# The last down projection of a two-model transformer kernel as seven block products in two passes, with the block sums on GpSimd

## What is computed

```
h2 = _rmsnorm(x, g_ffn[l])
z = _dwconv(h2 @ w_up[l], w_dw_ffn[l], b_dw_ffn[l])      # 2 * 2816 channels, taps -1, 0, +1 over tokens
zg, zv = jnp.split(z, 2, axis=-1)
x = x + (jax.nn.silu(zg) * zv) @ w_down[l]               # (512 x 2816) by (2816 x 1024)
...
return _rmsnorm(x, g_final)
```

## Time and profile before

| | |
|---|---|
| median of 3 runs | 1885.44 us (1885.15 to 1885.94) |
| span of the profiled execution (first to last instruction) | 1883.8 us; its own time outside the span is not given, the median of the runs lies 1.6 us above the span |
| busy: PE, DVE, ACT, POOL | 99%, 62%, 49%, 4% |
| last down projection on PE | 1754.2 to 1877.4 us, 123.2 us |
| last matmul started to end of span | 1877.2 to 1883.8 us |

### The profile page before, as it was taken

How to read it: one execution, slowest core, us unless ns; L and a number is a source line. 1 busy time by engine, 2 the same in 40 slices (tenths; PEclk the granted TensorE clock), 3 DMA queues, 4 the chain that set the end, 5 groups by cost and what they waited for, 6 DMA issues and landing times.

```text
span 1883.8 us, 27086 instructions
## 1 busy us (share of the span) xinstructions
PE 1861.2 (99%) x8985; PEld 1504.1 (80%) x8985; DVE 1165.4 (62%) x2030; ACT 917.1 (49%) x1685; POOL 75.4 (4%) x110
## 2 busy tenths in 40 slices
PE   8999999999999999999999999999999999999998
PEld 7888888888888877677888888888757878888887
DVE  6877765733333377776566666336777576666534
ACT  6777654543433353666544434334456553444433
POOL 1111000000000000100200000000010020000000
PEclk9999999999999999999999999999999999999999
DMA  5222232333333324521333333333441223333333
GB/s 153 69 79 79 76 104 79 101 95 100 95 98 97 95 73 102 108 53 35 101 95 95 95 95 105 96 95 88 118 83 43 68 81 109 95 95 95 96 95 106
DMA packets 169241, 171.33 MB, mean 91 GB/s; under 512 B 48563, under 2 KB 123329, under 8 KB 169153
## 3 DMA queue, kind: packets, MB, share of 16 engines
q1 hardware_dynamic: 169048, 170.16, 31.5%
q10 hardware_dynamic: 104, 0.03, 0.0%
HBM read 159.25 MB, written 2.10 MB: 86 GB/s over the span
## 4 chain that ended last, share of the span: by engine, by line
PE 91%; DVE 5%; ACT 2%; issue 1%; DMA 0%; SPq 0%; DVEq 0%; ACTq 0%
PE bank_b L2457 16%; PE bank_b L2458 16%; PE bank_b L2459 16%; PE bank_a L2457 11%; PE bank_a L2458 11%; PE bank_a L2459 11%; PE bank_b L2959 2%; PE bank_b L3063 2%; PE bank_a L3044 1%; DVE w_lo L1535 1%; DVE arena L1538 1%; DVE arena L1535 1%; PE bank_a L2482 1%; PE bank_a L2485 1%; PE bank_a L2488 1%
## 5 line engine op out<-in xcount | busy, mean ns | idle before, releaser
L1535 DVE TENSOR_TENSOR w_lo<-w_raw,w_hi 128x512 fp32r<-128x512 f32 (+2 forms) x621 | 412.3, 675 | 535.3 <-ACT w_hi L1264 327.4
L1264 ACT ACTIVATE w_hi<-w_raw 128x512 fp32r<-128x512 f32 (+3 forms) x396 | 232.9, 599 | 435.6 <-PE bank_b L2459 222.2
L2457 PE MATMUL bank_b<-h_hi,w_hi 128*128 128x512 f32 (+1 forms) x952 | 372.7, 391 | 1.9 <-DVE h_lo L1538 0.8
L2459 PE MATMUL bank_b<-h_hi,w_lo 128*128 128x512 f32 (+1 forms) x952 | 369.0, 388 | 0.0
L2458 PE MATMUL bank_b<-h_lo,w_hi 128*128 128x512 f32 (+1 forms) x952 | 369.0, 388 | 0.0
L901 ACT ACTIVATE w_hi<-w_raw 128x512 fp32r<-128x512 f32 x225 | 137.7, 627 | 227.6 <-PE bank_b L2459 116.9
L2457 PEld LDWEIGHTS bank_b<-h_hi,w_hi 128*128 128x128 f32 x952 | 178.8, 188 | 41.2 <-issue 3.1
L2458 PEld LDWEIGHTS bank_b<-h_lo,w_hi 128*128 128x128 f32 x952 | 178.8, 188 | 37.0 <-issue 1.4
L2459 PEld LDWEIGHTS bank_b<-h_hi,w_lo 128*128 128x128 f32 x952 | 178.7, 188 | 36.6
L2457 PE MATMUL bank_a<-h_hi,w_hi 128*128 128x512 f32 x513 | 200.6, 391 | 0.3
L2458 PE MATMUL bank_a<-h_lo,w_hi 128*128 128x512 f32 x513 | 199.5, 389 | 0.0
(11 more groups left out here) (314 smaller groups left out, 2665.3 us busy)
## 6 DMA issues: line engine op xcount, KB each, us to landing
w_raw<-in_w_up_dram SPq DMA_DIRECT2D x240, 256.0 KB, 3.1
w_raw<-in_w_down_dram SPq DMA_DIRECT2D x152, 256.0 KB, 2.6
arena<-arena SPq DMA_DIRECT2D x32, 268.0 KB, 4.2
w_raw<-in_w_in_dram SPq DMA_DIRECT2D x64, 128.0 KB, 2.3
w_raw<-in_w_gate_dram SPq DMA_DIRECT2D x32, 256.0 KB, 2.8
w_raw<-in_w_in_dram SPq DMA_DIRECT2D x32, 256.0 KB, 2.6
w_raw<-in_w_o_dram SPq DMA_DIRECT2D x32, 256.0 KB, 2.6
w_raw<-in_w_out_dram SPq DMA_DIRECT2D x16, 256.0 KB, 2.7
```

The lines of the kernel that those rows point to most:

```text
L1264: nc.scalar.activation(w_hi[:, s, 0:c], w_raw[:, s, 0:c], ACT.Copy).then_inc(w_round, 1)
L1535: return nc.vector.tensor_tensor(out_, a, b, op)
L2457: nc.tensor.matmul(out_, a_hi, b_hi, start=start, stop=False, skip_group_check=loose)
L2459: return nc.tensor.matmul(out_, a_lo, b_hi, start=False, stop=stop, skip_group_check=loose)
```

## The change

The down projection is written as a product of 2x2 blocks. Rows: tokens 0 to 255 and 256 to 511. Columns: the two halves of 512. The contraction is taken in 11 pairs q of chunks (2q, 2q+1). With x11, x21 the two token halves of `act2` tile 2q, x12, x22 those of tile 2q+1, and w11, w12, w21, w22 the four weight chunks of the pair, seven products of sums take the place of eight products of blocks. Each product is a chunk by two token tiles, so 6 matmuls; before, each of the eight blocks of a pair was that too.

- **Two passes.** PSUM holds only four accumulators of two banks (`acc_x`, `acc_v`, `acc_z`, `acc_y`). Pass 1 runs the products w11, t3, t2, t1 of all q, pass 2 w21, t4, w22. The order of all 77 products is `DOWN_ORDER`. Between the passes and within the second the accumulators are copied or added into SBUF (`copy_bank` on ACT, `tensor_copy` and `tt` on DVE, four adds on GpSimd). The residual is no longer put in first: four visits of eight transposes use `acc_y` in pass 2 and DVE adds them.
- **Sums on GpSimd.** `act_sums` makes three sums of 128x256 for each pair q out of `act2` (the ones of q = 0 to 8 during the up projection), `weight_sums` three of 128x512 for each q (t3 and t1 in place in the raw buffers, t2 into freed tiles), `second_sums` one of 128x256 and one of 128x512 for each q in pass 2.
- **Factors.** A factor is rounded by ACT (`round_factor`) and its rest made by DVE (`rest_factor`) into a ring of 8 slots instead of 4; an activation operand likewise (`round_unit`, `rest_unit`), still four slots. In pass 1 the units are two of 128x512 for each q, in pass 2 one of 128x512 and one of 128x256.
- **Loads.** 55 loads of 256 KB in place of 44 (w22 is loaded in both passes), into two raw buffers for each of w11, w12 and w22. A raw buffer is loaded again when the factor in it is split and t2 of that q is made (`pass1_freed`).
- **The last group's** FFN tiles are made between factors, its outer taps at q = 2 to 5 and its product at q = 6.
- **The end.** Token tiles 2 and 3 are finished first, then 0 and 1. Each output tile is a DVE add of PSUM and SBUF (`end_sum`) ahead of the squares, which now read SBUF.
- Semaphores are merged (`act_made`, `dve_set`, `raw_land`) with the same order of work.

```diff
+DP = F2T // 2
+HS = S // 2
+RING = 8
+PASS1, PASS2 = ("w11", "t3", "t2", "t1"), ("w21", "t4", "w22")
+DOWN_ORDER = ([(kind, q) for kinds in (PASS1[:2], PASS1[2:]) for q in range(2) for kind in kinds]
+              + [(kind, q) for q in range(2, DP) for kind in PASS1]
+              + [(kind, q) for kind in PASS2 for q in range(2)]
+              + [(kind, q) for q in range(2, DP - 2) for kind in PASS2]
+              + [("t4", DP - 2), ("t4", DP - 1)] + [(kind, q) for q in range(DP - 2, DP) for kind in ("w21", "w22")])
...
@@ sync
+            def pass1_freed(kind, q):
+
+                sp_.wait_ge(w_split, d0 + DOWN_AT[(kind, q)] + 1)
+                sp_.wait_ge(t_made, 3 * q + 3)
...
+            for q in range(DP):
+                for src, dst, slot, kind in ((last_down[:, 2 * q, 0, :], raw11, q % 2, "w11"),
+                                             (last_down[:, 2 * q, 1, :], raw12, q % 2, "t1"),
+                                             (last_down[:, 2 * q + 1, 1, :], raw22, 2 + q % 2, "t3")):
+                    if q >= 2:
+                        pass1_freed(kind, q - 2)
...
+                    sp_.dma_start(dst[q % 2], src).then_inc(raw_land[slot], 16)
@@ gpsimd
+            def act_sums(q):
+
+                x11, x21, x22 = act2[:, 2 * q, 0:HS], act2[:, 2 * q, HS:S], act2[:, 2 * q + 1, HS:S]
+                pool.wait_ge(a_ready, was[a_ready.name] + 2 * q + 2)
...
+                nc.gpsimd.tensor_tensor(s13_of[q][:, 0:HS], x21, x22, ALU.add).then_inc(s_made, 1)
+                nc.gpsimd.tensor_tensor(s13_of[q][:, HS:S], x11, x21, ALU.subtract).then_inc(s_made, 1)
+                pool.wait_ge(s_made, 3 * q + 2)
+                nc.gpsimd.tensor_tensor(x21, s13_of[q][:, 0:HS], x11, ALU.subtract).then_inc(s_made, 1)
+
+            def weight_sums(q):
...
+                nc.gpsimd.tensor_tensor(raw22[b], raw22[b], raw12[b], ALU.subtract).then_inc(t_made, 1)
+                pool.wait_ge(t_made, 3 * q + 1)
+                nc.gpsimd.tensor_tensor(raw12[b], raw12[b], raw11[b], ALU.subtract).then_inc(t_made, 1)
+                if q < 2:
+                    pool.wait_ge(w_split, d0)
+                else:
+                    pool.wait_ge(w_used, d0)
+                nc.gpsimd.tensor_tensor(t2_of[q], raw22[b], raw11[b], ALU.add).then_inc(t_made, 1)
+
+            def second_sums(q):
...
+                nc.gpsimd.tensor_tensor(act2[:, 2 * q, 0:HS], act2[:, 2 * q + 1, 0:HS], act2[:, 2 * q, HS:S],
+                                        ALU.subtract).then_inc(s_made, 1)
...
+                nc.gpsimd.tensor_tensor(raw12[r % 2], raw11[r % 2], t2_of[q], ALU.subtract).then_inc(t_made, 1)
...
+            for q in range(DP - 2):
+                act_sums(q)
+            weight_sums(0)
+            act_sums(DP - 2)
+            for q in range(1, DP):
+                weight_sums(q)
+                if q == DP - 3:
+                    act_sums(DP - 1)
@@ vector
+            for u in range(4):
+                rest_unit(u)
+            for kind, q in DOWN_ORDER[0:6]:
+                rest_factor(kind, q)
+            dve.wait_ge(w_used, d0)
+            for j in range(4):
+                tt(zp[:, j, 1:1 + S], bank_b[:, j, :], rstd[:, 1, :], ALU.mult).then_inc(z_out, 1)
+            for kind, q in DOWN_ORDER[6:8]:
+                rest_factor(kind, q)
+            for q in range(2, DP):
+                for kind in PASS1:
+                    rest_factor(kind, q)
+                for b in range(2):
+                    rest_unit(2 * q + b)
+                if 2 <= q < 6:
+                    for j in range(2):
+                        last_tap_of(2 * (q % 2) + j, 2 * (q // 4))
...
@@ tensor
+            def product(kind, q, acc, tiles, start, stop):
...
+                pe.wait_ge(w_split, d0 + n + 1)
+                pe.wait_ge(as_ready, before(DEPTH2 - 1)[as_ready.name] + u + 1)
+                for t in tiles:
+                    c = slice(first + t * P, first + t * P + P)
+                    last = mm3(acc[:, t, :], as_hi[:, u % 4, c], as_lo[:, u % 4, c], ring_hi(n), ring_lo(n), start, stop, True)
+                return last
...
+            def down_tokens(emptied):
...
+                for n, (kind, q) in enumerate(DOWN_ORDER[0:4 * DP]):
+                    if n == 4:
+                        pe.wait_ge(z_out, emptied + 4)
+                    product(kind, q, accs[kind], range(2), q == 0, q == DP - 1).then_inc(w_used, 1)
```

More of the change, by code:

```diff
@@ L1524, in _ @@
-            for t in range(TT):
-                for half in range(2):
-                    act.wait_ge(yt_made, 2 * t + half + 1)
-                    nc.scalar.activation(y_sq[:, 2 * t + half, :], y_bank(t, half), ACT.Square,
-                                         accum_out=tok[:, half, t:t + 1]).then_inc(tok_sq, 1)
-                tokens_guess(t, slice(t, t + 1))
+                act_pair(split2, act2, M_END - 4, F2T - 2, was["a_ready"])
+                for n in range(2):
+                    split_layer(l + 1, n)
@@ new lines, in _ @@
+            round_factor("w22", 1)
+            copy_bank(sum_p7, acc_v, ("t3", DP - 1))
+            for b in range(2):
+                round_unit(2 * DP + 2 + b)
+            for q in range(2, DP - 2):
+                for kind in PASS2:
+                    round_factor(kind, q)
+                for b in range(2):
+                    round_unit(2 * (DP + q) + b)
+                if q == 4:
+                    for t in range(2):
+                        act.wait_ge(yt_made, t + 1)
+                        nc.scalar.activation(sum_r[:, t, :], acc_y[:, t, :], ACT.Copy).then_inc(bank_copied, 1)
@@ new lines, in _, with token_square @@
+            for kind, q in (("t4", DP - 2), ("t4", DP - 1), ("w21", DP - 2), ("w22", DP - 2)):
+                round_factor(kind, q)
+            for q in range(DP - 2, DP):
+                for b in range(2):
+                    round_unit(2 * (DP + q) + b)
+            for kind in ("w21", "w22"):
+                round_factor(kind, DP - 1)
+            def token_square(src, half, t):
+                nc.scalar.activation(y_sq[:, 2 * t + half, :], src, ACT.Square,
+                                     accum_out=tok[:, half, t:t + 1]).then_inc(tok_sq, 1)
@@ L2437, in _, with rest_factor @@
-            dve.wait_ge(gain_land, 16)
-            for t in range(TT):
-                dve.wait_ge(tok_sq, TT + 2 * t + 2)
-                tokens_var(t, slice(t, t + 1))
-                tokens_rstd(t, slice(t, t + 1))
+                lo_pair(act2, m0 + M_END - 4, F2T - 2, was["as_round"])
+                for n in range(2):
+                    split_lo(m0 + M_END + n)
+            was = before(DEPTH2 - 1)
+            last_z = 4 * (F2G - 1)
+            def rest_factor(kind, q):
+                n = DOWN_AT[(kind, q)]
+                dve.wait_ge(w_round, d0 + n + 1)
+                rest(ring_lo(n), factor(kind, q), ring_hi(n)).then_inc(w_split, 1)
@@ new lines, in rest_unit, with last_tap_of @@
+            def rest_unit(u):
+                c = unit_cols(u)
+                dve.wait_ge(as_round, was[as_round.name] + u + 1)
+                rest(as_lo[:, u % 4, 0:c], unit(u), as_hi[:, u % 4, 0:c]).then_inc(as_ready, 1)
+            def last_tap_of(j, tap):
+                tile = 2 * (F2G - 1) + j % 2 + F2T * (j // 2)
+                c = L_FTAP + tap * 2 * F2T + tile
+                if tap == 0:
+                    dve.wait_ge(z_mid, was[z_mid.name] + last_z + j + 1)
+                else:
+                    dve.wait_ge(z_tap, was[z_tap.name] + last_z + j + 1)
+                ins = stt(cz[:, j, :], zp[:, j, tap:tap + S], cols_all[:, DEPTH2 - 1, c:c + 1], cz[:, j, :], ALU.mult, ALU.add)
+                ins.then_inc(z_conv if tap else z_tap, 1)
@@ new lines, in _, with end_sum @@
+            for kind, q in (("t4", DP - 2), ("t4", DP - 1), ("w21", DP - 2), ("w22", DP - 2)):
+                rest_factor(kind, q)
+            for q in range(DP - 2, DP):
+                for b in range(2):
+                    rest_unit(2 * (DP + q) + b)
+            for kind in ("w21", "w22"):
+                rest_factor(kind, DP - 1)
+            def end_sum(n, into, bank):
+                dve.wait_ge(yt_made, 8 + n + 1)
+                tt(into, bank, into, ALU.add).then_inc(end_summed, 1)
```

369 lines of the change are left out of this document (280 added, 89 removed).

## The result

The changed kernel took **1916.42 us** (median of 4 runs, 1915.88 to 1916.75) against 1885.3 for the kernel before (4 runs beside it): ratio 1.0165, with a 95% interval of 1.0152 to 1.0177. The prediction said slower, 1896.3 us, in a range of 1887 to 1910. The direction was right. The time lies 6.4 us above the range, and the loss is 31.1 us where 10.9 was forecast.

The account below looks back on a forecast made before the run. DVE and GpSimd, taking turns at SBUF, were to bound the down stage instead of PE: pass 1 ends at 1835.9, PE at 1885.6, plus 9.1 of end gives span 1894.7, plus 1.6 gives 1896.3 us; range 1887 to 1910.

Parts of the forecast that it names:

- the lock: In the down stage, GpSimd sums and DVE operations with two SBUF inputs exclude each other, so their costs add.
- the ledger: Adds DVE's steps and GpSimd's sums as one shared resource through the down stage, to a span of 1894.7 us.
- the price of 0.85 us: Cost to DVE of a 128x512 GpSimd sum not written over an input; sums written over an input cost 1.10.
- the order of GpSimd's queue: No cost was put for it; activation sums of q = 0 to 8 were to be covered by up-projection waits.
- nearly even: Pass 2: DVE with GpSimd takes 4.04 us a pair against PE's 4.08; PE ends at 1885.6, by its own work 1884.1.
- +2.7 us: After PE's end: an add of 0.7 us before the last square and about 2 us of another tile's work; 9.1 in all.
- evictions done: DVE is through with the evictions of the last up group at 1761.2 us, having come to them at 1758.8.
- pair 2 starts on PE: PE starts q = 2 of pass 1 at about 1769.4 us instead of 1765.1, after load, sums, rounding and rests.
- pair 10 starts: Pass 1, q = 3 to 10 at 6.65 us each plus taps, multiplications and activation sums, 61.1 us: start at 1830.5.
- PE's term: In the down stage, 462 matmuls instead of 528, at 0.2267 us each, take 15.0 us off PE.
- Rival 3: Something beyond the lock: two raw buffers' load loop, or a clock falling while PE waits; 1906 to 1915 us, chance 0.10.
- all at 1.10: Upper bound: all GpSimd sums from 1747.5 us at the dear price and no PSUM read hidden, 1906.5 us.

Follow-up runs that it names:

- tiny_sums: Changed kernel with every GpSimd sum of the down stage made on two columns, all else kept: 1878.19 us, ratio 0.9963 to the kernel before.
- tiny_weight: Changed kernel with only the 33 weight sums of pass 1 made on two columns: 1886.55 us, ratio 1.0008 to the kernel before.
- small_loads: Changed kernel with the 27 loads of pass 1 from pair 2 on bringing two columns instead of 512: 1914.97 us, ratio 1.0155 to the kernel before.
- late_end: Changed kernel with GpSimd's two groups of end sums two pairs later in its queue: 1913.73 us, ratio 1.015 to the kernel before.
- let_in: Changed kernel with DVE also waiting in pass 1, before its unit rests, for GpSimd's next t3 sum: 1918.16 us, ratio 1.0177 to the kernel before.
- dve_best: Changed kernel with all sums but pass 1's activation sums on DVE, factors 6 and 7 earlier, last adds reordered, last statistics joint: 1889.83 us, 1.0021 of the kernel before.

## Why the prediction was right and wrong

**Right.** The mechanism: PE does 462 matmuls of products and waits for DVE's rests, which a running sum stretches, one in 1.70 us, and the change loses. tiny_sums and tiny_weight show it. Loads, ACT and the eight slots are no bound (tiny_sums, small_loads). The prediction took without a row that DVE's PSUM reads don't meet the lock. They didn't: DVE adding two tiles out of PSUM, beside a GpSimd sum, both as quick as alone (0.60 a step, 1.29):

```profile
1875.24 1.28 DVE L1798 TENSOR_TENSOR arena<-arena,bank_b 128x512 f32<-128x512 f32 x2 [0.92 <-PE bank_b L3233]
```

```profile
1874.81 1.29 POOL L1039 TENSOR_TENSOR split_f<-ssum,h_hi_f 128x512 f32<-128x512 f32 x1 [4.10 <-DMA ssum<-in_w_down_dram]
```

**Wrong: the size.** Four terms of the ledger failed: the price of 0.85 us for t2 and t4 sums (1.10 measured), the order of GpSimd's queue, put at nothing (2.7 us by late_end, and a wait of 4.05 us at the start), pass 2 as "nearly even" (10.9 us over PE's own work), and the end, +2.7 us (+5.1 measured). Span against the ledger, 1914.2 against 1894.7; the first four rows are points in time, so each difference holds the one above it:

| | forecast | measured | difference |
|---|---|---|---|
| evictions done | 1761.2 | 1763.0 | 1.8 |
| pair 2 starts on PE | 1769.4 | 1772.05 | 2.65 |
| pair 10 starts | 1830.5 | 1837.6 | 7.1 |
| pass 1 ends on PE | 1835.9 | 1843.6 | 7.7 |
| pass 2 on PE | 49.7 us | 59.1 us | 9.4 |
| end | 9.1 us | 11.5 us | 2.4 |

- *Prices.* "0.85 for the others" was wrong: t2 sums show the cycle of 1.70 us like the in-place ones, and cost DVE 1.10. How quick a sum is by itself said nothing about what it costs in turn. A 128x256 sum cost DVE 0.54 (an operation beside one started 1.14 us ahead of the next, at 1816.21, less its own 0.60), not 0.45. The ledger at these prices: pass 1 is 8 x 0.25 + 0.25 more from q = 2 on, about 1.0 ahead of it, and pass 2 is 11 x (0.25 + 0.09) = 3.7 more. Together 7.0 us of the 17.1 up to PE's end.
- *Pass 2, "the two are nearly even there".* At 1.10 and 0.54 a pair is 4.38 us against PE's 4.08, which over eleven pairs would be 3.3 us. PE's 59.1 us are 10.9 above its own 48.2, and the trace shows no even stall: PE waits 1.0 us until 1846, 5.7 us until 1863.17 and 0.3 us until 1894, and nine slow matmuls cost 1.9 us; from 1874 to 1894 it is busy 19.96 of 20 us. Most of the loss is the one long wait, behind GpSimd's wait of 9.32 us for DVE's bank sum. The queue's order, which I never looked at for GpSimd, makes 2.7 us of it (late_end). I had told where DVE's PSUM adds stand, but not what is queued behind GpSimd's wait for them.
- *Start.* The evictions are 1.8 us late: DVE waits 4.05 us, until 1757.07, for ACT's rounding of t3 of pair 1, whose sum stands behind three activation sums in GpSimd's queue (rows under let_in). The ledger added durations and had neither latencies nor that order. What it costs wasn't tried.
- *PE's term.* 66 x 0.2267 = 15.0 us less is 12.3 in tiny_sums (1885.4 - 1878.2 + 5.1 for the longer end), in part because a matmul takes longer (below). It weighs fully only where PE is the bound.
- *The end*, "+2.7 us", measured +5.1 us: DVE is in the outputs of token tiles 2 and 3 until 1903.73 and only then adds, and two chains of statistics follow one another. dve_best shortens the end by 1.4 us.

From above the loss adds up: -15.0 + 2.7 (PE's term) + 5.1 (end) + 38.2 (sums) = 31.0 of 31.1. It has to, since the 2.7 and the 38.2 both come from tiny_sums. From below, prices 7.0, queue 2.7, end 2.4 and landings at most 1.5, PE's starts at most 2.7, give some 16 of the 19.5 us missing in the span. The last 3 to 4 are not settled; by the trace the 1.9 us of slow matmuls at 1863 and what the wait at the start costs beyond its 1.0 us of prices (pair 2 starts 2.65 us late) are of that size. The effects overlap, and a sum over them is not exact.

Rival 3 gave 1906 to 1915, nearer than the forecast, but by causes that the runs don't bear out: the loads' loop is worth at most some 1.5 us. The clock did fall, which I held unlikely (0.80 in one window), and cost some 1.9 us by the trace. That this range came near is luck.

The bound "all at 1.10", 1906.5, had the true price. It left out latency and queue order, the longer end and the clock, and stood 10 us low; the range reached to 1910 and was low too.

## What to carry to other kernels

Two engines that each have room by themselves may have none together: look in the trace of before for a place where both run, take the cycle of the pair as the price, for every form of the operation, and compare it with the idle time of the busier one. Such work is cheaper on DVE itself (0.60 us instead of 1.10), but then DVE's idle time is the budget, and here it did not suffice to win back the 15 us of matmuls. In a queue with sums for different purposes, put the one that waits longest behind those that nobody holds up, and one that nobody needs yet behind those that are awaited.
